# Scan levels 5 and 6 as block products and plain copies

## The reference

```
G = jnp.cumsum(gc, axis=-2)
rel = G[..., :, None, :] - G[..., None, :, :]
decay = jnp.exp(jnp.where(causal, rel, NEG_INF))
A = jnp.einsum('bhtk,bhsk,bhtsk->bhts', qc, kc, decay)
o = (jnp.einsum('bhts,bhsv->bhtv', A, vc)
     + jnp.einsum('bhtk,bhkv->bhtv', qc * jnp.exp(G), S))
```

## Time and profile before

| | us |
|---|---|
| median of 3 runs | 3305.74 |
| lowest and highest | 3304.07 and 3306.32 |
| the profiled execution, its own time | 3306.93 |
| span of its trace | 3304.9 |
| TensorE busy, share of the span | 2896.9, 88% |
| VectorE busy | 2588.3, 78% |
| ScalarE busy | 1714.5, 52% |

### The profile page before, as it was taken

The page is one execution under the profiler, slowest core; times in us unless marked ns, Lnnn a source line. Parts: engine busy times, 40 slices in busy tenths (PEclk is TensorE's granted clock), DMA queues, the critical chain, the costliest instruction groups (busy, mean ns, idle before and its releaser), DMA issues.

```text
span 3304.9 us, 37651 instructions
## 1 busy us (share of the span) xinstructions
PE 2896.9 (88%) x14041; PEld 2376.6 (72%) x14041; DVE 2588.3 (78%) x3916; ACT 1714.5 (52%) x2802; POOL 624.2 (19%) x533
## 2 busy tenths in 40 slices
PE   8999999999999999999999999997655441279998
PEld 7998998888888888888888888872222241157776
DVE  7786767776456878787556676689998899999998
ACT  6554555664444555555445674222434589645444
POOL 0000000000000000000000000375545333346664
PEclk9999999999999999999999999999887555589999
DMA  7555555555555555555556557999999999989998
GB/s 238 160 150 159 163 164 167 180 168 199 191 178 189 182 191 191 188 192 200 192 185 235 160 172 242 335 413 411 410 421 413 419 427 418 416 325 391 394 391 315
DMA packets 424909, 870.12 MB, mean 263 GB/s; under 512 B 18615, under 2 KB 248920, under 8 KB 391192
## 3 DMA queue, kind: packets, MB, share of 16 engines
q1 hardware_dynamic: 347776, 454.20, 41.1%
q0 software_dynamic: 75936, 413.17, 30.8%
q10 hardware_dynamic: 1016, 0.35, 0.0%
HBM read 865.56 MB, written 2.10 MB: 263 GB/s over the span
## 4 chain that ended last, share of the span: by engine, by line
PE 72%; DVE 12%; DMA 8%; issue 4%; ACT 2%; POOL 2%; DVEq 0%; SPq 0%; ACTq 0%; POOLq 0%
PE W L1792 15%; PE W L1843 12%; PE W L1845 12%; PE W L1844 12%; PE W L1789 8%; PE W L2010 5%; DMA Ub<-in_peer_u,ids 5%; DVE Ub L3197 5%; DVE X L3255 2%; PE T L2006 2%; DMA Vx<-in_peer_v,vid 2%; PE M L1896 2%; PE W L1747 1%; DMA Vr<-in_peer_v 1%; POOL Ub L3348 1%
## 5 line engine op out<-in xcount | busy, mean ns | idle before, releaser
L2746 DVE TENSOR_TENSOR wl<-raw,wh 128x1024 fp32r<-128x1024 f32 (+1 forms) x720 | 850.6, 1186 | 557.8 <-ACT wh L2150 556.1
L2150 ACT ACTIVATE wh<-raw 128x1024 fp32r<-128x1024 f32 (+1 forms) x720 | 740.7, 1031 | 887.3 <-PE W L1845 571.9
L1792 PE MATMUL W<-u,wh 128*128 128x512 f32 x2176 | 674.9, 396 | 1.3 <-DVE cw L2662 0.7
L3197 DVE CUSTOM_DVE_ANT_0 Ub<-Ub,W 128x2048 f32<-128x2048 f32 x226 | 511.8, 2283 | 27.3 <-DMA Ub<-in_peer_u,ids 19.5
L1789 PEld LDWEIGHTS W<-u,wl 128*128 128x128 f32 x2176 | 396.5, 188 | 87.6 <-issue 0.7
L1843 PE MATMUL W<-wh,u 128*128 128x512 f32 (+1 forms) x1152 | 436.4, 379 | 1.2 <-DVE u L3106 1.0
L1845 PE MATMUL W<-wh,u 128*128 128x512 f32 (+1 forms) x1152 | 428.2, 372 | 0.0
L1844 PE MATMUL W<-wl,u 128*128 128x512 f32 (+1 forms) x1152 | 427.7, 371 | 0.0
L1789 PE MATMUL W<-u,wl 128*128 128x256 f32 x2176 | 422.1, 280 | 0.3 <-DVE u L2708 0.3
L1982 PE MATMUL M<-Vx,diag 128*128 128x512 f32 x416 | 217.3, 674 | 144.2 <-DMA Vx<-in_peer_v,vid 88.5
L1792 PEld LDWEIGHTS W<-u,wh 128*128 128x128 f32 x2176 | 336.4, 189 | 7.0 <-DVE wl L2746 0.9
(11 more groups left out here) (405 smaller groups left out, 4587.4 us busy)
## 6 DMA issues: line engine op xcount, KB each, us to landing
raw<-in_w_in SPq DMA_DIRECT2D x128, 1024.0 KB, 5.1
raw<-in_w_up SPq DMA_DIRECT2D x88, 1024.0 KB, 4.8
Vr<-in_peer_v SPq DMA_DIRECT2D x128, 512.0 KB, 6.4
raw<-in_w_down SPq DMA_DIRECT2D x44, 1024.0 KB, 5.0
raw<-in_w_in SPq DMA_DIRECT2D x144, 256.0 KB, 3.4
raw<-in_w_out SPq DMA_DIRECT2D x32, 1024.0 KB, 5.0
raw<-in_w_proj_a SPq DMA_DIRECT2D x16, 1024.0 KB, 5.0
Wb<-in_peer_w_q SPq DMA_DIRECT2D x16, 1024.0 KB, 7.8
```

What stands on the lines that cost most here:

```text
L1792: return q.matmul(pr[h][:, :], H[:, k, col(h)], u[:, k0 + k, :, :].rearrange("p a t -> p (a t)"), start=first, stop=last)
L2150: q.activation(wh[:, s % NS, 0:b.half], r, ACT.Copy).then_inc(s_hi, 1)
L2746: q.tensor_tensor(wl[:, s % NS, 0:b.half], r, wh[:, s % NS, 0:b.half].bitcast(F32), SUB).then_inc(s_lo, 1)
L3197: q.tensor_tensor_reduce(U[:, :], U[:, :], inputs[:, :], 1.0, 0.0, MUL, ADD, dots[t][:, k:k + 1]).then_inc(s_dot, 1)
```

## The change

Three edits. In `scan_levels` levels 0 to 4 stay as they are; level 5 becomes two products of 32 left columns with 32 right columns, level 6 one product of 64 with 64. Each writes only its own piece of `M1`, on the partitions of its left tokens: 0 to 31 and 64 to 95 for level 5, 0 to 63 for level 6. In the built program these three carry a tile of the array of their own, 128 rows by 32 columns at column 0, the same at column 64, and 128 rows by 64 columns at column 0, where every other matmul of the kernel has 128 by 128. In `scan_sum` levels 5 and 6 become plain copies of these pieces. In the planner `scan_levels` is charged 1.6 us instead of 1.8.

```diff
@@ class Plan, scan_pair
-                t = self.done(("levels", hd, i), self.put("PE", 1.8, t, "scan_levels", hd, i))
+                t = self.done(("levels", hd, i), self.put("PE", 1.6, t, "scan_levels", hd, i))
@@ tensor, scan_levels
-                for lv in range(7):
+                for lv in range(5):
                     q.matmul((M0, M1)[lv // 4][:, col(lv % 4)], E[:, lv, cs], E[:, lv, cs], start=True, stop=True)
+                for lv, w in (5, 32), (6, 64):
+                    for o in range(0, P, 2 * w):
+                        left, right = slice(cs.start + o, cs.start + o + w), slice(cs.start + o + w, cs.start + o + 2 * w)
+                        c = P * (lv % 4) + o + w
+                        q.matmul(M1[o:o + w, c:c + w], E[:, lv, left], E[:, lv, right], start=True, stop=True)
@@ vector, scan_sum
-                    m = q.copy_predicated(a, hmask[:, lv, :].bitcast(U32), bank[:, col(lv % 4)])
+                    if lv in (5, 6):
+                        w = 1 << lv
+                        for o in range(0, P, 2 * w):
+                            c = P * (lv % 4) + o + w
+                            m = q.tensor_copy(a[o:o + w, o + w:o + 2 * w], bank[o:o + w, c:c + w])
+                    else:
+                        m = q.copy_predicated(a, hmask[:, lv, :].bitcast(U32), bank[:, col(lv % 4)])
```

## The result

| | before | changed |
|---|---|---|
| median, us | 3306.30 (8 runs) | 3315.05 (8 runs) |
| lowest to highest | 3302.82 to 3310.77 | 3312.15 to 3317.18 |
| profiled execution | 3306.93 | 3313.52 |
| span of its trace | 3304.9 | 3311.7 |

The changed kernel is slower: ratio 1.0025, 95% interval 1.0015 to 1.0034, 8.75 us between the medians. The forecast was 3315 us and slower.

What follows compares the result with a forecast made beforehand. TensorE was taken to bound the kernel: 3306.9 - 7.1 (products) + 15.7 (switches) + 0.5 (order) = 3316.0 us profiled, so a median of 3315 us. The range was 3299 to 3326 us, the forecast's own 3307 to 3321.

Steps and rivals of the forecast that it cites:

- What bounds the kernel: In the scan_levels stage TensorE's time is the time; a microsecond saved or added there moves everything behind it.
- The products: Levels 5 and 6 of scan_levels: six narrow records at 0.223 us replace 0.446 us, saving 7.1 us over 32 groups.
- The side-by-side case: Bound for level 5's two products: on different array columns they run together, saving 1.8 us more, 8.9 us in all.
- The estimate from the page on tiling: For the narrow records: 32 columns would cost what 60 do, making the 7.1 us saving about 4 us.
- The switches: Three changes of array width a group, 96 in all, each losing 0.164 us of record overlap: 15.7 us added.
- A full stop: Rival at each width switch: neither matmul nor weights enter early, 0.274 us each, 3325 us in all; chance 0.12.
- no loss: Rival at the width switches: narrow products follow wide ones as closely as wide ones do, 3299 us; chance 0.22.
- The order: Planner's 1.6 us moves heads and attention steps, with six more ScalarE table loads: 0.5 us added, bounds -0.2 and 2.
- The place with `oah` ahead and in blocks of 384 columns: One of two added places in the new order where ScalarE's logarithms and table loads delay TensorE; some 0.7 us at three.
- The copies: In scan_sum, three plain copies replace two predicated ones; a step of 2.61 us, hidden beside TensorE's work, so nothing.
- The sum: Whole kernel: 9.1 us more than before, median 3315 us, 0.28% slower.
- The distance of starts in a group: From a scan_levels group's first record to the weight product behind it: 1.71 us before, 1.98 us forecast.

Runs made afterwards that it cites:

- e12: e6 with the second level 5 product written to partitions 0 to 31, so both narrow products use the same array columns; ratio to before 1.0002, group 1.774 us.
- e7: Changed kernel with the planner back at 1.8 us and the products reordered for six width switches a group instead of three; ratio to before 1.0084, group 2.538 us.
- e1: Kernel before with only the planner's charge for scan_levels at 1.6 us instead of 1.8; ratio to before 1.0008, query start 2101.5 us.
- e9: Kernel before with fewer left and right columns in every level, full array width kept, no switch; ratio to before 0.9986, group 1.614 us.
- e3: Changed kernel, planner at 1.8 us, levels 5 and 6 each one product of all 128 left with 64 right columns; ratio to before 0.9999, group 1.785 us.
- e5: Kernel before with all seven levels multiplied with only their 64 right columns and all 128 left ones; ratio to before 1.0002, group 1.785 us.
- e6: Changed kernel with the planner at 1.8 us and the level 6 product left out; ratio to before 0.9998, group 1.718 us.
- e4: Kernel before with only the plain copies of level 5 and 6 pieces in scan_sum, products and planner as before; ratio to before 1.0000.
- e10: Kernel before with fewer left (stationary) columns in each level and all 128 right (moving) ones; ratio to before 0.9998, group 1.755 us.

## Why the prediction was right, step by step

**What bounds the kernel.** Right. Each kernel's query start moved by 32 times the change of its group, within 0.2 us and in e12 within 0.5 (e7: 24.1 us, 32 x 0.754 = 24.1), and by the order in e1 and the changed kernel.

**The products.** The price was nearly right: 0.028 us a record of 32 columns was forecast, and on the same columns of the array it is 0.032 (e12), while 64 columns were 0.056 as forecast (e9, at 65). The side-by-side case, which stood in the text as a bound, is what happens (e12): the narrow products cost 0.183 us instead of 0.223, so 0.26 us a group go and not 0.22, 8.4 us in all and not 7.1. The argument behind the price does not hold. It read 0.87 ns a column from the earlier trace rows, which are transposes (a product with the identity, `ident`), one record each, and took the fewer moving columns as the cause. Their stationary side has 128 columns all the same, and e3 and e5 show that for the products of `scan_levels` 64 moving columns instead of 128 give nothing. The weight loads differ; in before, of the transposes and of the level products:

```profile
L1685 PEld LDWEIGHTS W<-ident,cws x3: 139/139/141, 30.7 to 30.9; 88*128 88x128 f32 x3
L1896 PEld LDWEIGHTS M<-E x448: 187/192/193, 81.2 to 777.3; 128*128 128x128 f32 x150
```

A load of 128 columns lasts 0.14 us there and 0.19 us here, so a price of transposes could not be carried over to products. The forecast held since the narrow products also have fewer stationary columns, which is luck.

**The estimate from the page on tiling** (the Trainium skill, "TensorEngine Tiling (Array Packing)", section "Instruction Overhead"), by which a record of 32 columns would cost what 60 do, is not borne out in that form: 60 columns would be 0.052 us by the rate of the earlier trace rows, and e12 has 0.032. The Trainium skill gives the figure in cycles and as a number of columns. At the granted 2.4 GHz 60 cycles are 0.025 us, an estimate from its figure, while 0.87 ns a column are 2.1 cycles a column here, so the two part. A least time of 0.025 us would lie below the 0.032 us that a record of 32 columns takes on the same columns, and no run here has a shorter one. Between records on different columns it is no least distance: they start 7 ns apart (e6).

**The switches.** Right in kind and near in size: 0.152 to 0.160 us on average in four kernels, 0.164 forecast. Three a group are 0.46 us, 14.6 us in all, against 15.7. The make-up was wrong, and two errors cancel. The forecast took the whole overlap of 0.164 us as lost and the weight load as nothing, because two of three switches go into narrow weights. Measured are 0.094 us of the overlap at each switch, and 0.02, 0.05 and 0.10 us of weight load that nothing covers, which is most at the return to full width. The rule of the Trainium skill that a change of tiling mode drains TensorE (same page, "Key Properties") is borne out by e7, and e6 shows it for a change between 32 and 64 columns too; the share that the trace can give to it is the 0.094 us. A full stop (0.274 us) was too much, and no loss is refuted. Why the next record is held back by 0.094 us and not by all of 0.164 isn't shown.

**The order.** The step that was mis-sized: 0.5 us forecast, 2.4 us measured at the query start (e1), above the bound of 2 us. The place with `oah` ahead and in blocks of 384 columns, which the text named, costs what it warned of: by distances 0.68 - 0.17 + 2 x 0.11 = 0.73 us at 129 us. The text had priced such a place by its idle time of 0.21 us in the earlier trace rows; that one too costs 0.37 us by its starts (348.71 to 349.26, with 0.17 usual) and 0.11 behind it. Another 0.3 us go at 199 us, behind a table load as well. The largest, 1.36 us, is of another kind, `attn_values` last ahead of `out_v`, which the two orders side by side would have shown on PE and which the three places quoted did not.

**The copies.** Right: nothing (e4). A step of 2.61 us was forecast, and 2.65 measured.

**The sum.** -8.4 + 14.6 + 2.4 = 8.6 us, against 8.5 at the query start and 8.75 between the medians. The forecast of 9.1 us came from a group lengthened by 0.27 us where it is 0.19, and an order priced at 0.5 us where it is 2.4; the two errors, -2.4 and +1.9 us, cancel. So the sign and its cause, the switches, were right, and that the sum came out within 0.4 us is luck. The distance of starts in a group had been put at 1.98 us and measured 1.89.

## What to carry to other kernels

Where TensorE is the bound, count the changes of tile width in its instruction order before cutting a product down: here each costs 0.11 us on the way in and 0.20 us on the way back, 1 and 1.8 records of 128 columns, and it takes narrow products in a row to pay for it. Within the full width these float32 products got cheaper only where stationary and moving columns fell together, since the next product's weight load must fit under the stream of this one; a price read from transposes didn't carry over. A wait of TensorE is priced by the distance between starts, which here was 0.2 to 0.4 us more than the idle time at each place. A planner's constant that is corrected by 0.2 us changes the whole order, and its effect (0.07% here) can be more than a third of the edit's own.

## What had not been expected of the hardware

Two products of 32 stationary columns at columns 0 and 64 of the array take the time of one: their records start 7 ns apart (e6), and 32 ns apart on the same columns (e12). A switch of width has two prices, 0.094 us until the next record and 0.02 to 0.10 us for the weights, and they are the same within 1 ns in all 32 groups. Loads of 128 stationary columns hold float32 products 0.112 us apart even when only 64 columns are streamed (e5), and a stream of 128 columns holds them 0.109 us apart when less is loaded (e10), so in before the two limits lay almost on each other, and neither could be seen in its trace.
